# Delta-rule recurrence: outputs with features on partitions, and one matrix product per chunk for the mean of squares

## What is computed

```python
def _wkv7_scan(r, decay, k, v, a_in, b_in):       # per head, 64 x 64 state
    def step(S, inp):
        r_t, w_t, k_t, v_t, a_t, b_t = inp
        sa = jnp.einsum('bhij,bhj->bhi', S, a_t)
        S = (S * w_t[:, :, None, :] + sa[..., None] * b_t[:, :, None, :]
             + v_t[..., None] * k_t[:, :, None, :])
        y_t = jnp.einsum('bhij,bhj->bhi', S, r_t)
        return S, y_t
...
    y = _wkv7_scan(r, decay, k, v, -kk, kk * a)
    y = _layer_norm(y, lnx_g.reshape(A_HEADS, A_HEAD_DIM), lnx_b.reshape(A_HEADS, A_HEAD_DIM), GN_EPS)
    y = y + jnp.sum(r * k * r_k.astype(jnp.float32), axis=-1, keepdims=True) * v
    y = y.reshape(bsz, t, c).astype(x.dtype) * g
    return y @ w_o
```

## Time and profile before

| | us |
|---|---|
| median of 3 runs (lowest to highest) | 1311.26 (1311.18 to 1314.3) |
| the profiled execution | 1311.84 |
| its span in the trace | 1309.9 |
| TensorE busy | 1275.0 (97%) |
| VectorE busy | 894.4 (68%) |
| ScalarE busy | 679.8 (52%) |

### The profile page before, as it was taken

One profiled execution on the slowest core, in us unless ns is written; L12 is line 12 of the kernel. 1 busy time (PEld: TensorE's weight loads), 2 busy tenths in 40 slices (PEclk: granted clock), 3 DMA queues, 4 the chain that ended last, 5 costly groups with the idle time before them and its releaser, 6 DMA issues.

```text
span 1309.9 us, 24050 instructions
## 1 busy us (share of the span) xinstructions
PE 1275.0 (97%) x10247; PEld 1103.8 (84%) x10247; DVE 894.4 (68%) x1467; ACT 679.8 (52%) x1228; POOL 84.4 (6%) x103
## 2 busy tenths in 40 slices
PE   9999999999999999999999999999999999999997
PEld 6978888889967888888897997888887987788886
DVE  6886666673585665756998747676658466866676
ACT  6875544462494554544662534554544478445452
POOL 3000500000060000000001600000000000000000
PEclk9999999999999999999999999999999999999999
DMA  9445555544312555553343003655554441555550
GB/s 352 158 179 209 186 191 186 191 173 168 145 66 71 208 193 193 193 193 129 139 184 131 4 5 104 250 193 194 193 193 167 187 145 64 210 193 193 193 193 33
DMA packets 17498, 214.48 MB, mean 164 GB/s; under 512 B 1960, under 2 KB 2128, under 8 KB 4720
## 3 DMA queue, kind: packets, MB, share of 16 engines
q1 hardware_dynamic: 15888, 205.43, 42.8%
q0 software_dynamic: 1504, 7.52, 1.6%
HBM read 211.87 MB, written 1.06 MB: 163 GB/s over the span
## 4 chain that ended last, share of the span: by engine, by line
PE 81%; DVE 10%; ACT 6%; issue 1%; DMA 1%; SPq 0%; DVEq 0%; ACTq 0%
PE psum L695 25%; PE psum L669 13%; PE psum L675 7%; PE psum L485 4%; PE psum L486 4%; PE psum L487 4%; DVE w_low L1968 3%; ACT w_high L1414 2%; PE psum L1216 2%; PE psum L1057 1%; PE psum L1174 1%; PE psum L584 1%; PE psum L1344 1%; PE psum L580 1%; PE psum L1130 1%
## 5 line engine op out<-in xcount | busy, mean ns | idle before, releaser
L1968 DVE TENSOR_TENSOR w_low<-ring,w_high 128x1024 fp32r<-128x1024 f32 x372 | 443.3, 1227 | 193.3 <-ACT w_high L1414 193.3
L1414 ACT ACTIVATE w_high<-ring 128x1024 fp32r<-128x1024 f32 x372 | 372.7, 1048 | 127.0 <-PE psum L695 105.5
L695 PE MATMUL psum<-w_high,up_split 128*128 128x512 f32 x1024 | 287.6, 391 | 0.9 <-DVE up_split L2123 0.9
L695 PEld LDWEIGHTS psum<-w_high,up_split 128*128 128x128 f32 x1024 | 190.3, 188 | 40.6 <-issue 2.7
L669 PE MATMUL psum<-act_split,w_high 128*128 128x512 f32 x768 | 191.6, 391 | 0.0
L695 PE MATMUL psum<-w_low,up_split 128*128 128x512 f32 x512 | 163.2, 390 | 0.0
L669 PEld LDWEIGHTS psum<-act_split,w_high 128*128 128x128 f32 x768 | 139.6, 189 | 26.0
L485 PE MATMUL psum<-act_split,w_high 128*128 128x256 f32 x448 | 129.6, 289 | 0.0
L1515 ACT ACTIVATE up_split<-work 128x256 fp32r<-128x256 f32 x112 | 46.8, 418 | 159.4 <-DVE work L2116 148.8
L486 PE MATMUL psum<-act_split,w_high 128*128 128x256 f32 x448 | 126.7, 283 | 0.0
L487 PE MATMUL psum<-act_split,w_low 128*128 128x256 f32 x448 | 126.6, 283 | 0.0
(11 more groups left out here) (355 smaller groups left out, 1884.3 us busy)
## 6 DMA issues: line engine op xcount, KB each, us to landing
ring<-weights SPq DMA_DIRECT2D x95, 2048.0 KB, 7.7
work<-rows POOLq DMA_DIRECT2D x4, 1024.0 KB, 5.1
ring<-weights SPq DMA_DIRECT2D x4, 512.0 KB, 8.4
work<-rows POOLq DMA_DIRECT2D x4, 512.0 KB, 5.8
x<-x_in SPq DMA_DIRECT2D x2, 512.0 KB, 4.6
work<-t_bias POOLq DMA_DIRECT2D x1, 1024.0 KB, 7.6
out<-x SPq DMA_DIRECT2D x4, 256.0 KB, 2.1
con<-consts SPq DMA_DIRECT2D x1, 576.0 KB, 21.5
```

Of the source, the lines that this page charges most:

```text
L695: last = mm(bank(acc[(th, n)]), up_split[:, m, a, P * th:P * th + P], w[:, f], start=start and i == 0, stop=stop and i == len(pairs) - 1, ...
L1414: A(high[:, HIGH_SLOT[name], f], ring[:, n % RING, f], ACT.Copy).then_inc(weights_high, 1)
L1968: V.tensor_tensor(low[:, n % RING, f], ring[:, n % RING, f], high[:, HIGH_SLOT[name], f].bitcast(f32), ALU.subtract).then_inc(weights_spli ...
```

## The change

In the changed kernel y is computed with features on partitions and tokens along the row from the start: the two operands of its three products are swapped, and the results go to the half that belongs to the head (`by_head`). `turn_heads`, the sums of line 2600 and the multiplication of line 2605 are gone. In their place TensorE makes one product of the 128x128 constant `mean_head` (a 64x64 block of 1/64 for each head) with the 128x512 squares, `mean_squares`, which leaves the mean of squares on every partition of its head; ScalarE takes Ln and Exp of these 128x512 elements (`rstd`), and VectorE multiplies y by them (`heads_scaled`). `rstd(tc - 1)` stands on ScalarE between the copy of u and the square of chunk tc; `heads_scaled(tc - 1)` stands on VectorE ahead of `heads_out(tc - 1)`. The last `mean_squares` stands after k = 1 of the first 24 products with w_o, not after k = 4, and the last `rstd` between the first two quarters of rw_o1.

```diff
-            def turn_heads(tc):
+            def mean_squares(tc):
                 q = TURN[("wkv_turned", tc)]
                 open_bank(q)
-                read_out(pe, TURN[("wkv_y", tc)])
-                for c in range(NC):
-                    for hf in range(2):
-                        last = mm(psum[at_half(hf, tc), BANK[q], c * CH:c * CH + CH], y_norm[half(hf), c, :],
-                                  cst("diag")[half(hf), :], start=True, stop=True)
-                last.then_inc(bank_filled, 1)
+                pe.wait_ge(sig("gn_sq"), tc + 1)
+                mm(bank(q), cst("mean_head"), y_sq, start=True, stop=True).then_inc(bank_filled, 1)
...
-                opened = heads(y, [lambda at, hd, c: (rw_gk[at, c, tc, CH:2 * CH], units(RW_VT)[at, c, tc, :])], True, False)
+                opened = heads(y, [lambda at, hd, c: (units(RW_VT)[at, c, tc, :], rw_gk[at, c, tc, CH:2 * CH])], True, False, True)
...
-                    heads(y, [lambda at, hd, c: (rw_ar[hd, c, tc, 1, :], rw_s[hd, c, :])], False, False)
+                    heads(y, [lambda at, hd, c: (rw_s[hd, c, :], rw_ar[hd, c, tc, 1, :])], False, False, True)
...
-                    turn_heads(tc - 1)
+                    mean_squares(tc - 1)
...
-                heads(y, [lambda at, hd, c: (rw_gb[at, c, tc, CH:2 * CH], rw_u[at, c, :])], False, True)
+                heads(y, [lambda at, hd, c: (rw_u[at, c, :], rw_gb[at, c, tc, CH:2 * CH])], False, True, True)
...
-                        if (n, th, k) == (0, 0, 4):
-                            turn_heads(NT - 1)
+                        if (n, th, k) == (0, 0, 1):
+                            mean_squares(NT - 1)
...
+            def rstd(tc):
+                q = TURN[("wkv_turned", tc)]
+                filled(q)
+                taken(A(y_norm, bank(q), ACT.Ln, bias=gn_eps), q)
+                settle()
+                done(A(y_norm, y_norm, ACT.Exp, scale=-0.5), "gn_rstd")
...
-                done(A(y_norm.rearrange("p c i -> p (c i)"), bank(q), ACT.Square), "gn_sq")
+                if tc:
+                    rstd(tc - 1)
+                filled(TURN[("wkv_y", tc)])
+                done(A(y_sq, bank(TURN[("wkv_y", tc)]), ACT.Square), "gn_sq")
                 if tc:
                     heads_high(tc - 1)
-                act.wait_ge(sig("gn_var"), tc + 1)
-                done(A(y_var[:, tc, :], y_var[:, tc, :], ACT.Ln, scale=1.0 / DH, bias=gn_eps), "gn_log")
-                settle()
-                done(A(y_var[:, tc, :], y_var[:, tc, :], ACT.Exp, scale=-0.5), "gn_rstd")
-            split("rw_o1", [0, 1])
+            split("rw_o1", [0])
+            rstd(NT - 1)
+            split("rw_o1", [1])
             heads_high(NT - 1)
...
+            def heads_scaled(tc):
+                q = TURN[("wkv_y", tc)]
+                dve.wait_ge(sig("gn_rstd"), tc + 1)
+                filled(q)
+                taken(V.tensor_tensor(y_norm, bank(q), y_norm, ALU.mult), q)
+                settle()
...
                 if tc:
+                    heads_scaled(tc - 1)
                     for i in range(2):
                         heads_out(tc - 1, i)
-                dve.wait_ge(sig("gn_sq"), tc + 1)
-                done(V.tensor_reduce(y_var[:, tc, :], y_norm, AX.X, ALU.add), "gn_var")
-                if tc:
                     heads_low(tc - 1)
-                q = TURN[("wkv_y", tc)]
-                dve.wait_ge(sig("gn_rstd"), tc + 1)
-                taken(V.tensor_tensor(y_norm, bank2(q, NC), view(y_var[:, tc, :], [[1, NC], [0, CH]]), ALU.mult), q)
             split("rw_o1", [0])
+            heads_scaled(NT - 1)
             for i in range(2):
                 heads_out(NT - 1, i)
```

More of the change, by code:

```diff
@@ L291, in build @@
         y_raws = [work[:, i, :].rearrange("p (c s t) -> p c s t", c=4, s=2) for i in (10, 15)]
-        y_norm = work[:, RW_X, 1536:2048].rearrange("p (c i) -> p c i", c=NC)
-        y_var = small[:, 256:288].rearrange("p (n c) -> p n c", n=NT)
+        y_sq, y_norm = work[:, RW_X, 1536:2048], small[:, 0:512]
         v_split = over("v_split", 6, [P, NC, 2, T])
@@ L1822, in _ @@
                 taken(A(rw_u.rearrange("p c i -> p (c i)"), bank(q), ACT.Copy), q)
-                q = TURN[("wkv_y", tc)]
-                filled(q)
-                done(A(y_norm.rearrange("p c i -> p (c i)"), bank(q), ACT.Square), "gn_sq")
+                if tc:
+                    rstd(tc - 1)
+                filled(TURN[("wkv_y", tc)])
+                done(A(y_sq, bank(TURN[("wkv_y", tc)]), ACT.Square), "gn_sq")
                 if tc:
                     heads_high(tc - 1)
-                act.wait_ge(sig("gn_var"), tc + 1)
-                done(A(y_var[:, tc, :], y_var[:, tc, :], ACT.Ln, scale=1.0 / DH, bias=gn_eps), "gn_log")
-                settle()
-                done(A(y_var[:, tc, :], y_var[:, tc, :], ACT.Exp, scale=-0.5), "gn_rstd")
-            split("rw_o1", [0, 1])
+            split("rw_o1", [0])
+            rstd(NT - 1)
+            split("rw_o1", [1])
             heads_high(NT - 1)
@@ L2559, in _ @@
             dve.wait_ge(sig("g_scaled"), NC)
+            def heads_scaled(tc):
[4 more added lines that the diff above has]
+                settle()
             def heads_out(tc, i):
-                q = TURN[("wkv_turned", tc)]
                 c, t = slice(4 * i, 4 * i + 4), slice(tc * CH, tc * CH + CH)
                 raw = y_raws[i][:, :, 1, t]
[L2566 to L2572, removed]
+                step(V.tensor_tensor(raw, y_norm.rearrange("p (c t) -> p c t", c=NC)[:, c, :], chunks(RW_G)[:, c, t],
+                                     ALU.mult))
                 settle()
```

## The result

The changed kernel takes 1314.67 us (median of 20 runs, 1313.28 to 1316.11), the kernel before 1312.08 us (20 runs, 1309.94 to 1314.3). The ratio is 1.0017, with a 95% interval of 1.001 to 1.0023: 1.3 to 3.0 us slower, some 2.2 (the two medians lie 2.59 us apart). I had forecast a loss of 1.34 us, a change within 0.3%. It is a loss and within 0.3%, but larger than forecast, and 1314.67 lies outside my range (1310.7 to 1314.0). A part of that distance is the base: the three runs that I had started from gave 1311.26, twenty give 1312.08, which is 0.82 us more. On that base the forecast would have been 1313.4, and 1.25 us would still be missing.

A forecast was written before the change was run, and what follows sets the result against it. TensorE, busy 97% of the span, was taken as the bound. Tail 1.0, two mean products 0.5, copy of g 0.06, idle piece -0.22 gave +1.34 us: span 1311.24, median 1312.6, range 1310.7 to 1314.0.

The forecast's parts named there:

- The tail: From the end of u of chunk 3 to the second tokens: the longer ScalarE and VectorE chain loses 1.0 us.
- nine links: Steps on ScalarE and VectorE from the end of u, 789.52, to TensorE's second tokens at 800.25, before 799.24.
- Rival (a): Second tokens: the tail is covered and TensorE's own sum decides, +0.46 us, 1310.7 to 1311.7; chance 0.20.
- the price of the turns inside the recurrence: TensorE: a 1.18 us product replaces each 0.93 us turn, 0.25 us dearer each, 0.75 us for three.
- The idle piece of 0.44 us: Unexplained TensorE idle time in the recurrence: fewer products could shrink it, bounds 0 and -0.44 us, taken as -0.22.
- The idle piece of 0.56 us: Unexplained TensorE idle time beside the tail's chain: its going would count for nothing.
- The last term of the sum: From profiled execution to median: the profiled 1311.84 us lies 0.58 over the median 1311.26, so 1313.2 becomes 1312.6.
- The copy of g: ScalarE, chunk 3: scaling delays it but Ln and Exp leave its path, so TensorE's wait grows by at most 0.06 us.
- Rival (b): Chunks 2 and 3: scaling delays the copy of g by 0.73 us each, 1.46 us more, 1314.0; chance 0.11.
- Rival (c): Second tokens: idle TensorE has its clock halved, 24 products take 12 us, not 6, giving 1318.6; chance 0.04.

The follow-up runs named there:

- the run that took 0.94 us out of the chain: Changed kernel with the first quarter of rw_o1 moved behind the norm of chunk 3: start of u to second tokens 10.65 us in place of 11.59.
- the short turns: Kernel before with the turns of chunks 0 to 2 cut from 16 products to 2: state additions 8.09 us apart, 8.59 before.
- the runs with the mean product: Kernel before with one 128x512 product by mean_head replacing the turns of chunks 0 to 2, ScalarE and VectorE work unchanged: period 9.10 us, 8.59 before.
- the other quarters: Kernel before with the turns of chunks 0 to 2 written to the other half of the partitions: period 8.83 us, 8.59 before.

## Why the prediction was right and wrong

**The tail held.** I had put the first product of the second tokens 10.7 us behind the end of u of chunk 3, by a sum of nine links; from the mean product, which follows that end, it is 10.5. In the trace of after (ScalarE, then VectorE):

```profile
792.10 0.69 ACT L1815 ACTIVATE small<-psum,nst 128x512 f32<-128x512 f32 x1 [0.45 <-PE psum L1197]
792.82 0.63 ACT L1817 ACTIVATE small<-small 128x512 f32<-128x512 f32 x1
...
796.24 1.05 ACT L1409 ACTIVATE w_high<-ring 128x1024 fp32r<-128x1024 f32 x1
797.19 0.67 ACT L1815 ACTIVATE small<-psum,nst 128x512 f32<-128x512 f32 x1
797.89 0.63 ACT L1817 ACTIVATE small<-small 128x512 f32<-128x512 f32 x1
```

```profile
793.48 0.69 DVE L2568 TENSOR_TENSOR small<-psum,small 128x512 f32<-128x512 f32 x1 [3.70 <-ACT small L1817]
794.21 0.42 DVE L2575 TENSOR_TENSOR work<-small,work 128x256 f32<-128x256 f32 x1
...
798.56 0.69 DVE L2568 TENSOR_TENSOR small<-psum,small 128x512 f32<-128x512 f32 x1
...
800.88 0.42 DVE L2584 TENSOR_TENSOR y_split_a<-work,y_split_a 128x256 fp32r<-128x256 f32 x1
```

Ln takes 0.69 and Exp 0.63 us, as reckoned from the 128x8 forms. From the mean of chunk 2 (790.93) to the second tokens (801.44) it is 10.51 us, 0.8 more than the 9.72 of before (1.0 forecast). Rival (a), that the tail is covered, falls with the wait of 1.76 us and with the run that took 0.94 us out of the chain.

**The step that failed is the price of the turns inside the recurrence**, "so each of three turns becomes dearer by 0.25 us". The new product was priced rightly: 0.86 + 0.32 = 1.18 forecast, 1.16 measured. The old turn was not. I took 0.93 us from chunk 3, the only place in the earlier trace rows where a turn stands clear of its neighbours, and held it for all three. In chunks 1 and 2 the turn lies on the quarters of the array that the state's products leave free and costs 0.57 us, by the short turns and by the count of records alike; on the same quarters it costs the 0.93 us of the forecast. The period thus grows by 0.51 us, not by 0.25. The sign was in rows 2: the records of L1200 and L1216 alternate from 781.74, and do not at 789.52. The 0.91 us that the prediction took for a block have the same flaw: the row from 776.26 to 781.74 holds 188 records, not six full blocks, so a block there takes 0.93.

**The idle piece of 0.44 us was given a value that it didn't have**, -0.22 us. It went, as I thought it might, and nothing was gained. In chunk 2 of the kernel before, where the piece stands, the copy of g ended at 779.97 and u started at 780.05 (counted by records), so u could not have come earlier by much. In chunk 3, from the last state addition to u, it is 4.84 us before (783.70 to 788.54), 4.84 after (785.01 to 789.85), and 4.84 in the runs with the mean product and with the other quarters: the chain state, gate, high half, copy of g sets that distance, and TensorE merely waits elsewhere in it.

The idle piece of 0.56 us was rightly given nothing, as the low half sets the time after. But it is a part of the 37.18 us of before, where TensorE doesn't wait between that piece and the second tokens. From the start of u it takes 10.70 us to them there, and 10.25 in the run with the other quarters, which has the same order on TensorE and 0.12 us of that piece. What makes the two pieces stays open; against an execution of before without the second one the loss would be larger by almost half a us.

Together: u of chunk 3 was to start 0.34 us later and starts 1.07 us later (27.55 - 26.48): some 0.5 from two turns sized wrongly, 0.22 from the idle piece. With the tail's 0.9 us from there that is the 1.96. The times themselves lie 2.2 to 2.6 us apart; where the rest comes from I have not located. The last term of the sum was off too: I took the median of before to lie 0.58 us under its profiled execution, and by twenty runs it lies 0.24 over it. In a range moved by these 0.82 us (1311.5 to 1314.8) the 1314.67 would lie, so that it falls outside is owed to the base as well; the sizes above are read between marks and don't depend on it.

**The copy of g held** in one sense (its 0.06 us measured nothing): it comes 4.21 us after the state, as before (787.91 - 783.70 and 789.22 - 785.01), since Ln and Exp, which no longer stand ahead of it, freed what the scaling took. Rival (b), 0.73 us more on each copy, falls. The sign that I gave for it, a wait for the copy of g well over 0.31 us, was a bad one: the waits are 0.46 and 0.56 us, and the copy is no later behind the state; TensorE reaches it sooner, without the idle piece. But the place is a bound all the same: putting the copy first takes out 1.24 us.

**Rival (c)**, a clock that falls behind the wait at the second tokens, didn't happen: the stretch from there to 810 us has a granted clock of 1.00 behind an idle time of 1.76 us. It does fall at other idle pieces, which both kernels share.

```profile
801.44:810.00 8.56, 8.56 (x38) 7.11 (x39) 7.92 (x10) 4.64 (x5) 0.00 (x0) 1.00 0.23 59
```

## What to carry to other kernels

A matrix product's price is read at the place where it stands, with its neighbours: on a TensorE that runs 64x64 products, the same sixteen cost 0.57 us beside work on the other quarters of the array and 0.93 beside work on the same ones, and a single 128x128 product among them pays 0.3 us for the two changes of shape. Fewer instructions on the busiest engine are no gain by themselves; first find the loop that joins the engines (here state, gate, copy of g, u, state), and ask which links the new work adds to it. And where two engines keep their work in a fixed order, weight preparation that stands in such a chain costs its full length: moving one quarter out of it gave back 0.94 of 1.96 us.

## What the runs showed of the hardware

The granted clock falls to its lower level in some executions and not in others at the same idle piece of the same program: behind 2.18 us of idle TensorE near 1118 us it stayed at 1.00 before, and it was 0.79 on the mean of the stretch from 1118 to 1126 us after, where the end of the span came 1.4 us later for it. The page of before shows 9 in all its 40 slices, that is 90% or more, and not the full level throughout: in finer stretches the clock is 0.83 from 10 to 20 us and from 1080 to 1090 us there. In two executions it fell at the start of the recurrence (0.83 over 10 us), where no other did. Falls of this size are one source of the spread of one kernel's times (1309.94 to 1314.3 us for before); whether they are all of it is not shown. Changes of 1 us are to be read between marks of a trace.
